# Even layer of a two-block model: sliding attention taken head by head between the weight products, on one core

## The reference, cut to what matters

```python
def even_layer(hn, w_in, gla_w_up, gla_b_up, gla_gain, sinks, w_out, rel_bias):
    proj = hn @ w_in
    aq, ak, av, a_down, a_gate, bq, bk, bv, b_gate = split_cols(proj, EVEN_SPLITS)
    log_a = jax.nn.log_sigmoid(a_down @ gla_w_up + gla_b_up) / GLA_TAU
    oa = gla_chunked(aq, ak, av, log_a)        # 4 heads, key 64, value 128, chunks of 64 tokens
    oa = rmsnorm_2(oa, gla_gain) * jax.nn.silu(a_gate)
    ob = swa_attention(bq, bk, bv, sinks, rel_bias) * jax.nn.silu(b_gate)   # 8 heads of 64, window 128
    return jnp.concatenate([oa, ob], axis=-1) @ w_out
```

## Time and profile before

| What | us |
|---|---|
| median of 3 runs | 1112.95 |
| lowest and highest run | 1109.2, 1115.51 |
| the profiled execution's own time | 1105.91 |
| its span in the profile | 1104.1 |
| TensorE busy in the span | 1016.8 |
| VectorE, ScalarE, GpSimd busy | 709.9, 520.6, 291.5 |

### The profile page before, as it was taken

How to read it: one execution, slowest core, us unless ns; L and a number is a source line. 1 busy time by engine, 2 the same in 40 slices (tenths; PEclk the granted TensorE clock), 3 DMA queues, 4 the chain that set the end, 5 groups by cost and what they waited for, 6 DMA issues and landing times.

```text
span 1104.1 us, 19306 instructions
## 1 busy us (share of the span) xinstructions
PE 1016.8 (92%) x6824; PEld 886.7 (80%) x6824; DVE 709.9 (64%) x1105; ACT 520.6 (47%) x881; POOL 291.5 (26%) x273
## 2 busy tenths in 40 slices
PE   7887999898999999989889999999998978899876
PEld 2476743477999999978779999999998954799765
DVE  0588667764888877677876655545555526465673
ACT  1344333353766444444544666644436514454552
POOL 0335400111899311130041376611100001110022
PEclk9988888999899999999999999999999955699998
DMA  7646533324987877669535555555554510055500
GB/s 273 240 175 218 190 141 102 116 72 149 334 284 268 288 261 278 221 226 331 185 131 170 167 183 188 185 176 190 171 184 153 172 38 1 27 165 174 170 1 39
DMA packets 54761, 194.26 MB, mean 176 GB/s; under 512 B 5935, under 2 KB 8399, under 8 KB 54320
## 3 DMA queue, kind: packets, MB, share of 16 engines
q1 hardware_dynamic: 54304, 192.10, 50.3%
q0 software_dynamic: 400, 1.39, 0.4%
HBM read 192.39 MB, written 1.07 MB: 175 GB/s over the span
## 4 chain that ended last, share of the span: by engine, by line
PE 79%; DVE 11%; ACT 4%; issue 3%; DMA 2%; POOL 1%; SPq 0%; DVEq 0%; ACTq 0%; POOLq 0%
PE bank L427 21%; PE bank L429 21%; PE bank L428 21%; PE bank L520 2%; DVE w_lo L1243 2%; ACT w_hi L889 2%; PE bank L752 2%; PE bank L614 1%; PE bank L613 1%; PE bank L733 1%; PE bank L631 1%; DVE tile_f L1283 1%; PE bank L622 1%; DMA raw<-weights 1%; PE bank L741 1%
## 5 line engine op out<-in xcount | busy, mean ns | idle before, releaser
L1243 DVE TENSOR_TENSOR w_lo<-raw,w_hi 128x1024 fp32r<-128x1024 f32 x259 | 334.9, 1296 | 156.4 <-ACT w_hi L889 155.4
L889 ACT ACTIVATE w_hi<-raw 128x1024 fp32r<-128x1024 f32 x259 | 272.5, 1054 | 172.5 <-PE bank L429 151.5
L427 PE MATMUL bank<-act_hi,w_hi 128*128 128x258 f32 (+1 forms) x872 | 250.0, 287 | 9.3 <-DVE w_lo L1243 6.5
L428 PE MATMUL bank<-act_lo,w_hi 128*128 128x258 f32 (+1 forms) x872 | 246.7, 283 | 0.0
L429 PE MATMUL bank<-act_hi,w_lo 128*128 128x258 f32 (+1 forms) x872 | 246.6, 283 | 0.0
L427 PEld LDWEIGHTS bank<-act_hi,w_hi 128*128 128x128 f32 x872 | 165.8, 190 | 11.5 <-DVE w_lo L1243 6.7
L428 PEld LDWEIGHTS bank<-act_lo,w_hi 128*128 128x128 f32 x872 | 166.0, 190 | 1.0 <-issue 1.0
L429 PEld LDWEIGHTS bank<-act_hi,w_lo 128*128 128x128 f32 x872 | 165.8, 190 | 0.0
L428 PE MATMUL bank<-hid_lo,w_hi 128*128 128x256 f32 x512 | 145.2, 284 | 0.0
L429 PE MATMUL bank<-hid_hi,w_lo 128*128 128x256 f32 x512 | 145.2, 284 | 0.0
L427 PE MATMUL bank<-hid_hi,w_hi 128*128 128x256 f32 x512 | 145.2, 284 | 0.0
(11 more groups left out here) (308 smaller groups left out, 1866.5 us busy)
## 6 DMA issues: line engine op xcount, KB each, us to landing
raw<-weights SPq DMA_DIRECT2D x259, 512.0 KB, 3.4
ada_raw<-ada SPq DMA_DIRECT2D x96, 512.0 KB, 4.7
bias<-bias_by_distance SPq DMA_DIRECT2D x1, 2048.0 KB, 8.1
x<-x_in SPq DMA_DIRECT2D x1, 1024.0 KB, 7.2
ctx<-ctx_in SPq DMA_DIRECT2D x1, 1024.0 KB, 8.5
out<-result SPq DMA_DIRECT2D x1, 1024.0 KB, 3.9
ws<-gm_ws POOLq DMA_DIRECT2D x1, 512.0 KB, 4.6
sq<-gm_rows POOLq DMA_DIRECT2D x1, 512.0 KB, 5.8
```

Of the source, the lines that this page charges most:

```text
L427: pe.matmul(dst, w[0], a[0], start=start, stop=False)
L428: pe.matmul(dst, w[0], a[1], start=False, stop=False)
L889: act.activation(w_hi[:, slot, :], raw[:, slot, :], ACT.Copy).then_inc(weight_hi, 1)
L1243: dve.tensor_tensor(w_lo[:, slot, :], raw[:, slot, :], w_hi[:, slot, :].bitcast(fp32), ALU.subtract).then_inc(weight_lo, 1)
```

## The change

The projections of the even layer are put in another order: `even_s` (6 chunks: `bk`, `bv`, `bq` 4), `even_bg` (4 gate chunks of the sliding attention), then `even_a` (5), `even_av` (4), `even_ag` (4 gate chunks of the linear attention), `even_out`. The weight rows of the host arrays follow, and `even_out` takes the sliding attention's part of its input first.

A beat b is one step of the sliding attention: scores of head b, transposes of head b - 1, values of head b - 2. Beats 0 to 4 each stand behind one chunk of `even_a`, beats 5 to 8 behind one of `even_av`, beat 9 behind the first of `even_ag`. On VectorE a beat is evacuation, logits and maxima of both halves of head b, the weight conversion, then both normalisations and for odd b from 3 on a tile; on ScalarE a conversion, the copies of head b - 1, the exponentials of head b. The factors of the linear attention are made between beats (`z` after beat 1, `cum` after beat 3, exponentials after beats 4 and 5, `qe`, `ke`, `kl` after beat 6). Its products stand behind the chunks of `even_ag`: scores behind the first, key-value products behind the second, outputs behind the third. The column sums, two half groups of `even_out`, the spread, two more half groups and the other halves follow; the remaining four groups run whole. PSUM banks of these stages come from `banks_of_groups`: the beats use banks 4 and 5 for scores, 6 for transposes, 2 for values, while `even_a` alternates between 0 and 1, and `even_av` has 3 and 7. `logit` and `prob` get memory of their own, `state` shares that of `z` and `zl`.

```diff
@@ stages and banks
-    ("even_a", [1] * 5), ("even_av", [0, 0, 0, 2]), ("even_b", [1] * 14), ("even_out", [1] * 8),
+    ("even_s", [1] * 6), ("even_bg", [1] * 4), ("even_a", [1] * 5), ("even_av", [0, 0, 0, 2]),
+    ("even_ag", [1] * 4), ("even_out", [1] * 8),
+FOUR_BANKS = {'even_s': 'even_s', 'even_bg': 'even_s'}
+TOKEN_BANKS = {'even_av': (3, 7)}
+OUT_BANKS = ('even_out',)
+            if name in FOUR_BANKS:
+                banks.append((n - count.group0[FOUR_BANKS[name]] + 2) % 4)
+            elif name in TOKEN_BANKS:
+                banks.append(TOKEN_BANKS[name][g])
+            elif name in OUT_BANKS:
+                banks.append((0, 1, 3, 7)[g % 4])
+            else:
+                banks.append(n % 2)
@@ memory
-            o_gla, logit, prob = e_last, e_pos, e_neg
+            o_gla = e_last
+            logit = sb("logit", [P, 2, S], fp32, even)
+            prob = sb("prob", [P, 2, S], fp32, even)
@@ TensorE
+            def late(name, a, groups, ks=range(KT), a_wait=None, a_sem=split_lo):
+                for g in groups:
+                    n, c = group0[name] + g, chunk0[name] + g
+                    if ks[0] == 0:
+                        pe.wait_ge(weight_lo, c + 1)
+                        if bank_free[n]:
+                            pe.wait_ge(evacuated, bank_free[n])
+                    for k in ks:
+                        if a_wait is not None:
+                            pe.wait_ge(a_sem, a_wait(k))
+                        last = split_product(bank[bank_of[n]][:, 0:S], weight(c, k * P, P), a(k), k == 0, k == KT - 1)
+                    if ks[-1] == KT - 1:
+                        last.then_inc(matmul_steps, 1)
+            def beat(att_, heads, b, probs, turned, part, paired, i0):
+                if b < H:
+                    q, k_, _ = heads(b)
+                    if b >= 2:
+                        pe.wait_ge(att_.logits, 2 * b - 2)
+                    for qt in range(2):
+                        pe.matmul(bank[4 + b % 2][:, unit(qt)], q[:, qt * P:(qt + 1) * P], k_[:, 0:(qt + 1) * P],
+                                  start=True, stop=True).then_inc(att_.scores, 1)
+                if 1 <= b <= H:
+                    if b >= 2:
+                        pe.wait_ge(att_.turned_read, 2 * b - 2)
+                    for u in (2 * b - 2, 2 * b - 1):
+                        pe.wait_ge(att_.normed, u + 1)
+                        for kt in range(u % 2 + 1):
+                            last = pe.transpose(bank[6][:, (u % 2 + kt) * P:(u % 2 + kt + 1) * P],
+                                                probs[:, u % 2, kt * P:(kt + 1) * P], ident)
+                        last.then_inc(att_.turned, 1)
+                if b >= 2:
+                    h = b - 2
+                    slot = h // 2 if paired else h
+                    pe.wait_ge(att_.turned_read, 2 * h + 2)
+                    if slot >= 1:
+                        pe.wait_ge(split_src, written(i0 + slot - 1))
...
+            for g in range(5):
+                late("even_a", act, [g])
...
+                if g == 1:
+                    pe.wait_ge(masks_in, 32)
+                    pe.wait_ge(evacuated, group0["even_a"] + 1)
+                    for t in range(2):
+                        pe.matmul(bank[7][:, t * S:(t + 1) * S], w_up[:, t * P:(t + 1) * P], down[:],
+                                  start=True, stop=True).then_inc(g_z, 1)
+                window_beat(g)
+            pe.wait_ge(g_z_ready, 2)
+            for j in range(4):
+                project_tokens("even_av", [j], TOKEN_BANKS["even_av"], act, 2, 512, chunks_all=4)
+                window_beat(5 + j)
...
+            late("even_out", even_o, range(2), range(4), a_wait=even_o_wait)
             pe.wait_ge(g_rstd, 1)
...
+            late("even_out", even_o, range(2, 4), range(4))
+            late("even_out", even_o, range(4), range(4, 8), a_wait=even_o_wait)
+            late("even_out", even_o, range(4, 8))
@@ ScalarE
             for g in range(5):
                 convert(chunk0["even_a"] + g + 4)
+                window_beat(g)
+                if g == 2:
+                    act.wait_ge(g_z_ready, 2)
...
+            for g in range(4):
+                act.wait_ge(evacuated, group0["even_ag"] + g + 1)
+                act.activation(gate[:, g, :], gate[:, g, :], ACT.Silu).then_inc(gated, 1)
             root(rms_gla[:], bank[6][0:H, 0:P], P, g_sums, 1, g_std)
@@ VectorE
+            for g, dst in enumerate([down[:], aq[:, 0, :], aq[:, 1, :], ak[:, 0, :], ak[:, 1, :]]):
+                evacuate("even_a", g, dst, rows=16 if g == 0 else P)
+                window_logits(g)
+                convert(chunk0["even_a"] + g + 4)
+                window_rest(g)
```

More of the change, by code:

```diff
@@ L768, in _, with unit @@
[L768 to L776, removed]
+            def unit(qt):
+                return slice(qt * P, qt * P + (qt + 1) * P)
@@ new lines, in beat @@
+            def beat(att_, heads, b, probs, turned, part, paired, i0):
[21 more added lines that the diff above has]
+                        pe.wait_ge(split_src, written(i0 + slot - 1))
+                    v = heads(h)[2]
+                    for qt in range(2):
+                        for kt in range(qt + 1):
+                            last = pe.matmul(bank[2][part(h), qt * P:(qt + 1) * P], v(kt),
+                                             turned[:, (2 * h + qt) % 4, kt, :], start=kt == 0, stop=kt == qt)
+                    last.then_inc(att_.values, 1)
@@ new lines, in window_beat @@
+            def window_beat(b):
+                beat(window, window_heads, b, prob, prob_t, pair, True, split0["even_o"])
+            raw_start("even_s", "even_in", 4, 2)
+            late("even_s", act, range(1, 4))
+            pe.wait_ge(evacuated, group0["even_s"] + 2)
+            for tt in range(2):
+                pe.transpose(bank[7][:, tt * P:(tt + 1) * P], bv[:, tt * P:(tt + 1) * P],
+                             ident).then_inc(v_turned, 1)
+            late("even_s", act, range(4, 6))
@@ L789, in _ @@
[L789 to L814, removed]
-                            last = pe.matmul(bank[4 + h % 2][:, at_:at_ + 64], state[pair(h), n - 1, h // 2, :],
-                                             qe[pair(h), h // 2, n * 64:(n + 1) * 64], start=False,
-                                             stop=n == 2 * tt + 1)
-                last.then_inc(g_o, 1)
+                    pe.wait_ge(window.logits, 2 * H)
@@ new lines, in _ @@
+            for j in range(4):
+                convert(chunk0["even_av"] + j + 4)
+                window_beat(5 + j)
+                if j == 0:
+                    for t in range(2):
+                        for n in range(4):
+                            tok = slice(n * 64, (n + 1) * 64)
+                            ins = act.activation(e_last[:, t, tok], cum[:, t, tok], ACT.Exp, scale=-1.0 / TAU,
+                                                 bias=decay[:, 0, t, n:n + 1])
+                    ins.then_inc(g_exp, 1)
@@ new lines, in _, with window_logits @@
+            for j, dst in enumerate([bk[:], bv[:], bq[:, 0, :], bq[:, 1, :], bq[:, 2, :], bq[:, 3, :]]):
+                evacuate("even_s", j, dst)
+                convert(chunk0["even_s"] + j + 4)
+            for g in range(4):
+                evacuate("even_bg", g, gate[:, 4 + g, :])
+                convert(chunk0["even_bg"] + g + 4)
+            def window_logits(b):
+                if b < H:
+                    beat_logits(window, logit, True, 0.125, lambda h: (h % 2) * 4 + h // 2, b)
```

334 lines of the change are left out of this document (219 added, 115 removed).

## The result

The changed kernel takes 1078.9 us (median of 4 runs, 1078.01 to 1080.95) against 1111.56 of the kernel before beside it (4 runs): a ratio of 0.9718, 95% interval 0.9685 to 0.9752. In a second series it took 1078.84 against 1112.03, ratio 0.969, interval 0.9664 to 0.9716. The forecast was 1079.5. The changed kernel's profiled execution took 1078.26, span 1076.5.

What follows compares the result with a forecast made beforehand. TensorE's chain bounds the kernel, with 70.2 us of small attention work near half clock. 74.9 us replaced by 37.4 saves 37.5, less 4 for the clock: 1105.9 - 33.5 = 1072.4, with the offset 1079.5; range 1069 to 1096.

Steps and rivals of the forecast that it cites:

- the prediction's sign: In the beats: granted clock 1.00, listed among the signs that would show the forecast right.
- Step 1 and 2: Sliding attention in beats: TensorE sets a beat at 4.97 us with its chunk, VectorE right behind at 4.8.
- Step 3: Queues followed beat by beat: one-off work makes TensorE wait in beats 4, 5, 7 and 8, together 7.2 us.
- Step 4: Linear attention behind gate chunks: waits of 4.6 and 3.0 us vanish, outputs take 6.3, half of 12.5.
- rival (c): Half clock from first beat to output projection: +65 us, 1140; with anything else giving back all, 0.05 slower, 0.03 same.
- Step 5: Tail before the output projection: squares' wait, sums and staggering 3.4 us; root's wait and spread 3.3 us.
- The clock: Falls in linear attention outputs and tail: 4 us allowed, between nothing and 8, cutting 37.5 saved to 33.5.
- the bound of 8: Upper clock cost: falls in outputs and tail, each up to 2 us on what is left, 2 on next chunk.
- the 7.05 us between profile and median: Whole kernel before: profiled execution 1105.9 against median 1112.95; same offset added to 1072.4 to give 1079.5.
- (a): Beats held by VectorE's strict order: a beat 7 us rather than 5.6, +12, time 1091; chance 0.15.
- (b): Clock falls in each beat's gap and each chunk lifts it: 2.5 x 9 = +22, time 1101; chance 0.09.
- (d): No clock lost and waits hidden: 37.5 to 41 us saved, 1072 to 1075.5; chance 0.08.

Runs made afterwards that it cites:

- the kernel with filling: Kernel before the change plus 128 unread 256-column TensorE products, eight before each transpose step of the sliding attention: 1110.37 us, ratio 1.0017.

## Why the prediction was right, and where its terms were off

The direction, the mechanism and the range were right. That the median came within 1 us of the forecast is luck: the profiled execution was forecast at 1072.4 and took 1078.3, 5.9 more, of which 3.9 lie in the even layer and 3.4 in the odd one, less 1.4 in the stages ahead.

**The mechanism.** Forecast: the 70 us of small work at half clock are replaced by work between chunks at the full clock. The granted clock in the beats is 0.97, nine beats took 50.5 us (forecast 50.6), and putting the beats in a block gave back 10 us. Shown, as an average: the prediction's sign was a clock of 1.00, and one of the nine beats lost it.

**Step 1 and 2, the beat.** TensorE was to set the beat with 4.97 a full one, VectorE with 4.8 right behind. TensorE's busy time over the nine was 46.99. Of that 1.6 is one fall of the clock (value products 1.51 for 0.84, the chunk after them 3.90 from 872.78 to 876.68, where the one before took 2.98). The remaining 45.4 are 5.04 a beat, against (50.6 - 7.2) / 9 = 4.82 in the forecast: 2.0 us more over nine beats. It goes to the joints: a full beat without a wait takes 5.32 us (850.77 to 856.09), 2.28 for the small products where 2.1 were forecast and 3.04 for the chunk where 2.87 were.

**Step 3, the waits.** The sizes were 1.7, 2.0, 1.1 and 2.2 in beats 4, 5, 7 and 8, together 7.2. Measured: 0.9 in beat 4, 2.0 in beat 5, none in 7 and 0.6 in beat 8, together 3.5. Here is ScalarE's and VectorE's part of beat 4:

```profile
856.77 1.28 ACT L1280 ACT_TABLE_LOAD   x1
858.07 0.63 ACT L1280 ACTIVATE z_state<-z_state 128x512 f32<-128x512 f32 x1
...
860.10 1.28 ACT L1060 ACT_TABLE_LOAD   x1
861.39 0.40 ACT L1060 ACTIVATE prob<-logit,small 128x128 f32<-128x128 f32 x1
```

```profile
863.78 0.69 DVE L1784 SCALAR_TENSOR_TENSOR z_state<-z_state 128x512 f32<-128x512 f32 x1
864.50 1.70 DVE L1785 TENSOR_TENSOR_SCAN cum<-masks,z_state 128x512 f32<-128x512 f32 x1
```

The table loads are back to back with their neighbours, as in the earlier trace rows, 1.28 each. The Trainium skill's drain of 1.38 us for each load (ScalarE: Activation LUTs, What ACT_TABLE_LOAD costs) shows nowhere here: the next instruction starts 0.02 after 1.28 us. Its single set for exp and ln (the same page, Table sets: the hidden batching unit) wasn't used either; there is a load before Ln and one before Exp.

The one-off work on VectorE stands where it was put. The waits of beats 7 and 8 mostly didn't come: VectorE had caught up in beat 6, where it waits 2.2 us for scores. A likely reason is that the fall of the clock in beat 5 held TensorE back by 1.6 us and the joints by another 0.2 a beat; no run without that fall exists to show it. Less waiting and more work cancelled, which is why the sum of the beats came out to 0.1 with two terms off by 3.7 one way and 2.0 + 1.6 the other. The agreement of the sum says less than it seems.

**Step 4, the outputs.** Forecast 6.3, half of 12.5. Two mistakes: at the full clock they take 7.1 (1.77 for each head, 901.97 to 905.50 for two), since not all of a small product's time halves with the clock; and the clock fell after 3.5 of them. Measured 9.75, outside the 6 to 9 that the prediction named as a sign of being right. The same error sits in the price of rival (c): weight products start 0.21 us apart at half clock and 0.12 at the full one (912.10 to 915.51, 915.88 to 916.35), so a chunk at half clock takes 5.1 us and not 5.7.

**Step 5, the tail.** Squares and sums 3.48 (forecast 3.4), wait and spread 3.2 (forecast 3.3: 1.09 and 2.09). Right.

**The clock.** This is the term that was mis-sized: an allowance of 4 us, between bounds of 0 and 8. It fell at three places, and it cost 2.6 in the outputs, 2.0 on the chunk behind them, 1.2 at the start of the output projection's later groups and 1.6 in beat 5: 7.4, near the bound of 8 that the prediction named and passed over. The bound counted a fall in the outputs and one in the tail; that in beat 5 it had not foreseen. The rows it had spoke for the outputs: they had been at 0.50 throughout.

**The odd layer and the total.** The even layer saved 29.6 in the profiles where 33.5 were forecast. Of the difference of 3.9, worked out from the terms above, the clock is 3.4, the outputs' own pace 0.8, the joints in the beats 2.0 and the shorter waits -3.7; the stretch of the gates from 889.14 to 901.97 took 12.8 against 12.2 of listed work (0.6), the nine chunks ahead of the beats 26.3 against 25.8 (0.5), and the column sums and biases before these 3.1 against 3.7 (-0.6). That is 3.0; 0.9 is not placed.

The odd layer was 3.4 longer in that execution; another execution of the same kernel shows 110.4. The medians differ by 32.7 in one series and 33.2 in the other, more than the 29.6 to 29.8 of the even layer. Only one profile of the kernel before exists, 6 to 7 us faster than its medians. The clocks on record say what sets it apart: its mean granted clock is 0.935, and in the eleven runs of the second series it is 0.925 to 0.929. With two levels, 1.00 and 0.50, the share of time at half clock is twice what the mean lacks to 1.00. At 0.928 a run of 1110 us spends an estimated 2 x 0.072 x 1110 = 160 us at half clock, the profiled one 2 x 0.065 x 1104 = 144. So the usual execution of the kernel before loses the clock for some 16 us more than its profile shows, and where it does so is left open. The changed kernel's runs have 0.953 to 0.956, its profile 0.955. The forecast carried the 7.05 us between profile and median over, and the changed kernel's profile lies only 0.6 under its own median; the 5.9 us that it was too low and this offset cancelled.

**The rivals.** (a) VectorE's order holding the beats: no, 3.5 us of waits. One evacuation is late, `ak` in beat 4, 4.8 us after its chunk's last product ended, and TensorE didn't wait for it:

```profile
866.32 0.42 DVE L1450 TENSOR_TENSOR ak<-bank,rstd 128x256 f32<-128x256 f32 x1
```

With two banks for the chunks ahead of the beats there is still no wait for an evacuation. (b) A swing of the clock in every beat: one in nine. (c) Half clock throughout: no; the block of beats shows what it looks like, 0.54, and even that kept 19.7 of the even layer's 29.6 us. (d) Nothing lost: no.

## What to carry to other kernels

Small attention products cost twice when they ran by themselves here, once for the waits between their steps and once for the clock that fell; put between weight chunks, one head at a time, they cost little more than their own length. Outputs cut into pieces of 3.5 us and less kept the clock here, 9.75 in a row did not, and part of the price is paid by the dense work that follows. When a forecast sum meets the measurement, compare its terms before trusting them; and look at the granted clock of the profiled execution beside those of the other runs before taking a difference between the two as fixed.

## What the runs showed of the hardware that was not expected

- TensorE can be busy without a pause and still lose its clock. The outputs of the linear attention are back to back from 901.97 on (busy 9.75 of 9.75) and go from 2.4 to 1.2 GHz at 905.5; split into pieces of 3.5, 1.7 and 1.7 us between weight products they stay at 1.00. Short pieces are no warrant: behind the sums, two half groups of dense products and the spread, each 1.8 to 2.9 us long, the clock fell for 3.4 us in every profile of the changed kernel and its variants, and no run here took that fall away.
- With 256-column products put between the small ones the block began with 10.3 us at 0.50, of which 8.4 lie behind the first of these products (912.97 to 921.36), until 1.00 was granted; then it held. Dense weight products alone had lifted it after 4.0 us.
- The same wait of 2.83 us was followed by products at 1.00 in the profile of the kernel before and by 5.7 us at 0.50 in that of the kernel with filling, with the same instructions up to there.
- The odd layer has two lengths, 110.3 and 113.8 us, with 6.8 or 17.1 us at half clock, in executions of the same kernel and whatever the even layer did. What decides it was not found.
- The scan took 1.70 us in beat 4, and 1.22 where no GpSimd work lay beside it (in the kernel before, and with the beats in a block). The scan in the kernel before:

```profile
834.23 1.22 DVE L1587 TENSOR_TENSOR_SCAN cum<-masks,z 128x512 f32<-128x512 f32 x1
```

  And the row of GpSimd's timeline in the changed kernel, to be read beside its scan at 864.50 above:

```profile
864.40 0.72 POOL L1894 TENSOR_TENSOR oe_lo<-tile_f,oe_hi 128x256 fp32r<-128x256 f32 x1 [51.01 <-ACT oe_hi L1000]
```

  GpSimd reads and writes SBUF until 865.12, 0.62 us after the scan began. The Trainium skill (SBUF — State Buffer, SBUF: two separate sides) has the two engines share a port, which an operation of VectorE with two inputs in SBUF must wait for when one of GpSimd that reads SBUF came first: by that the scan would show 1.22 + 0.62, an estimate of 1.84. The trace agrees in direction and nearly in size; no run took only the GpSimd operation away.
